# Index keys and head weights of the second layer: weight columns stationary, tokens moving

## The reference, cut to what matters

```python
h = _rmsnorm(x, ln_mix_g[l])
proj = h @ w_in[l]
(aq, ak, av, iq, ik, iw, hq, ...) = _split_cols(proj)
...
wi = wi * (IDX_HEADS ** -0.5 * IDX_DIM ** -0.5)
...
sc = jax.nn.relu(jnp.einsum('bqhd,bsd->bqhs', qi_b, ki))        # 4 heads x 64
sc = jnp.einsum('bqhs,bqh->bqs', sc, wi_b).astype(jnp.float32)
...
_, idx = lax.top_k(sc, n_sel)
```

## Time and profile before

| what | value |
|---|---|
| median of the timed runs | 1281.21 us |
| the three runs | 1283.12, 1279.31, 1281.21 us |
| profiled execution, from its first to its last instruction (span) | 1275.6 us |
| the profiled execution's own time as a run | not listed beside the span |
| PE busy | 1195.1 us (94%) |
| DVE / ACT / POOL busy | 642.8 / 478.1 / 207.0 us |
| product `ikw`, from its first matmul to that of `akv` | 784.97 to 792.80 us |
| product `akv`, from its first matmul to that of `aq` | 792.80 to 806.16 us |

### The profile page before, as it was taken

The page is one execution under the profiler, slowest core; times in us unless marked ns, Lnnn a source line. Parts: engine busy times, 40 slices in busy tenths (PEclk is TensorE's granted clock), DMA queues, the critical chain, the costliest instruction groups (busy, mean ns, idle before and its releaser), DMA issues.

```text
span 1275.6 us, 16095 instructions
## 1 busy us (share of the span) xinstructions
PE 1195.1 (94%) x6536; PEld 854.7 (67%) x6536; DVE 642.8 (50%) x949; ACT 478.1 (37%) x741; POOL 207.0 (16%) x190
## 2 busy tenths in 40 slices
PE   7998999999988998999999988999999889999998
PEld 7986754344435986654444435889887767988996
DVE  3897631212125678712222116596489885445544
ACT  3596421111103466311010113475566534444442
POOL 6000000000002000000000000087788550000000
PEclk9999989999999999789999998999999999999999
DMA  9900879999998531789999993533334342264450
GB/s 332 331 1 1 332 294 431 426 428 428 426 420 280 195 140 59 292 371 427 427 428 427 428 406 130 198 132 133 132 136 176 140 144 79 119 238 159 181 215 33
DMA packets 68162, 321.23 MB, mean 252 GB/s; under 512 B 4071, under 2 KB 12660, under 8 KB 55418
## 3 DMA queue, kind: packets, MB, share of 16 engines
q1 hardware_dynamic: 64944, 308.57, 61.1%
q0 software_dynamic: 2592, 11.42, 2.6%
q10 hardware_dynamic: 554, 0.23, 0.1%
HBM read 317.02 MB, written 3.18 MB: 251 GB/s over the span
## 4 chain that ended last, share of the span: by engine, by line
PE 70%; DVE 15%; DMA 5%; ACT 4%; issue 3%; POOL 2%; DVEq 0%; SPq 0%; ACTq 0%
PE bank L1529 32%; PE bank L1712 23%; PE bank L1594 4%; PE bank L1703 3%; DMA arena<-in_moe_w_up_dram 2%; POOL w_lo L666 2%; DMA ring<-in_w_kv_dram 2%; PE bank L1761 2%; DVE w_lo L666 2%; PE bank L1497 1%; ACT w_hi L953 1%; DVE arena L2298 1%; DVE rows L2852 1%; DVE arena L2871 1%; PE bank L1601 1%
## 5 line engine op out<-in xcount | busy, mean ns | idle before, releaser
L666 POOL TENSOR_TENSOR w_lo<-ring,w_hi 128x512 fp32r<-128x512 f32 (+1 forms) x124 | 178.1, 1469 | 659.3 <-ACT w_hi L953 659.3
L953 ACT ACTIVATE w_hi<-ring 128x2048 fp32r<-128x2048 f32 (+1 forms) x102 | 191.9, 1883 | 213.0 <-PE bank L1529 211.5
L666 DVE TENSOR_TENSOR w_lo<-ring,w_hi 128x2048 fp32r<-128x2048 f32 x71 | 160.8, 2266 | 150.4 <-ACT w_hi L953 149.9
L1529 PE MATMUL bank<-x_hi,w_hi 128*128 128x256 f32 x672 | 112.0, 289 | 3.9 <-DVE x_lo L2253 2.2
L1529 PE MATMUL bank<-x_hi,w_lo 128*128 128x256 f32 x672 | 108.9, 284 | 1.2 <-POOL w_lo L666 1.0
L1529 PE MATMUL bank<-x_lo,w_hi 128*128 128x256 f32 x672 | 108.3, 284 | 0.0
L1529 PE MATMUL bank<-w_hi,x_hi 128*128 128x512 f32 (+1 forms) x336 | 96.7, 403 | 10.8 <-DVE x_lo L2633 3.6
L1712 PE MATMUL bank<-arena 128*64 128x512 f32 x352 | 98.6, 594 | 1.9 <-ACT arena L953 1.8
L1529 PE MATMUL bank<-w_lo,x_hi 128*128 128x512 f32 (+1 forms) x336 | 94.4, 396 | 4.3 <-POOL w_lo L666 4.3
L1529 PEld LDWEIGHTS bank<-x_hi,w_hi 128*128 128x128 f32 x672 | 93.2, 193 | 6.5 <-issue 6.0
L953 ACT ACTIVATE arena<-bank 128x512 f32<-128x512 f32 (+3 forms) x85 | 40.0, 486 | 148.5 <-PE bank L1745 103.9
(11 more groups left out here) (333 smaller groups left out, 1776.9 us busy)
## 6 DMA issues: line engine op xcount, KB each, us to landing
ring<-in_w_in_dram SPq DMA_DIRECT2D x15, 2048.0 KB, 7.8
ring<-in_moe_w_gate_dram SPq DMA_DIRECT2D x12, 2048.0 KB, 20.0
arena<-in_moe_w_down_dram SPq DMA_DIRECT2D x12, 2048.0 KB, 21.8
arena<-in_moe_w_gate_dram SPq DMA_DIRECT2D x12, 2048.0 KB, 17.1
ring<-in_moe_w_down_dram SPq DMA_DIRECT2D x12, 2048.0 KB, 18.4
ring<-in_moe_w_up_dram SPq DMA_DIRECT2D x12, 2048.0 KB, 17.6
arena<-in_moe_w_up_dram SPq DMA_DIRECT2D x12, 2048.0 KB, 21.4
wslots<-in_moe_w_up_dram SPq DMA_DIRECT2D x8, 2048.0 KB, 22.5
```

The costliest lines, as they stand in the source:

```text
L666: last = ops.tensor_tensor(part(w_lo, label, hb)[:, x].bitcast(F32R), ring_half(label, hb)[:, x], part(w_hi, label, hb)[:, x], ALU.subtract)
L953: return s.activation(dst, src, ACT.Copy)
L1529: last = mm(bank(use_)[:, at:at + cols], still, moving, start=start and opens and (hb, n, k) == (0, 0, 0), stop=stop and closes and (hb, n ...
```

## The change

The product `ikw` is made with the 68 weight columns stationary and all 256 tokens moving, in one unit instead of two, into partitions 0 to 67 of one bank. ACT copies the 64 key rows out of it twice, to partitions 0 to 63 and 64 to 127 of `ikT`, and the 4 weight rows into a new tile `iwT`; these three copies stand in ACT's program behind both `w_hi` of `akv` and ahead of `w_hi` half 0 of `aq`. PE transposes the two 4-row pieces of `iwT` back (4 columns each) where it transposed `ikd`, and DVE scales them out of PSUM into `iws` behind the remainders of `hf`. The five DVE operations and the tiles `ikw` and `ikd` go, and so does ACT's copy of `ikT`. In `split_product` the signal `hi_read` moves, for a product with one unit only, from the last matmul of the second term to the first of the third. Nine semaphores are folded into others that are counted on; no instruction is added by that.

```diff
-        add("ikw", wide(win, C_IK, IKW), IKW, ("ikw", NT - 1))
+        add("ikw", wide(win, C_IK, IKW), IKW, ("ikw", 0))
...
             highs("akv")
+            ready(act, ("ikw", 0))
+            for twice in range(2):
+                copy(ikT[twice * HD:(twice + 1) * HD, :], bank(("ikw", 0))[0:HD, 0:T])
+            free(copy(iwT[HD:IKW, :], bank(("ikw", 0))[HD:IKW, 0:T]), ("ikw", 0))
             high("aq", 0)
...
             free(copy(iqT, bank("iqT")[:].rearrange("p (c t) -> p c t", c=2)), "iqT")
-            ready(act, "ikT")
-            free(copy(ikT, bank("ikT")[:, 0:T]), "ikT")
...
-                            last = mm(bank(use_)[:, at:at + cols], still, moving,
+                            last = mm(bank(use_)[0:still.shape[1], at:at + cols], still, moving,
                                       start=start and opens and (hb, n, k) == (0, 0, 0),
                                       stop=stop and closes and (hb, n, k) == (1, 2, rows_ - 1))
-                        if n == 1 and closing:
+                            if n == 2 and k == 0 and opening and closing:
+                                last.then_inc(hi_read[hb], 1)
+                        if n == 1 and closing and not opening:
                             last.then_inc(hi_read[hb], 1)
...
-                    pe.wait_ge(sem("ikd"), 1)
-                    pieces("ikT", [lambda t: ikd[:, t, :]])
+                    claim(pe, "iwT")
+                    freed(pe, ("ikw", 0))
+                    for t_ in range(NT):
+                        last = tr(bank("iwT")[:, t_ * IDX_HEADS:(t_ + 1) * IDX_HEADS], iwT[HD:IKW, t_ * P:(t_ + 1) * P],
+                                  ident[HD:IKW, HD:IKW])
+                    full(last, "iwT")
...
-            linear_tok("ikw", "ikw", IKW, arrives="rm0")
+            split_product("ikw", [(("ikw", 0), T, slice(0, T), slice(0, IKW))], False, arrives="rm0")
             linear_tok("akv", "akv")
             linear_tok("aq", "aq", steps=during_aq)
-            for label in ("iqT", "ikT"):
-                freed(pe, label)
+            freed(pe, "iqT")
...
             low(dve, v, "akv", 0)
-            for t in range(NT):
-                ready(dve, ("ikw", t))
-                free(v.tensor_copy(ikw[:, t, :], bank(("ikw", t))[:, 0:IKW]), ("ikw", t))
-            freed(dve, ("ikw", NT - 1))
-            v.tensor_scalar(iws, ikw[:, :, HD:HD + IDX_HEADS], IDX_HEADS ** -0.5 * HD ** -0.5, None, ALU.mult)
-            v.tensor_copy(ikd[:, :, 0:HD], ikw[:, :, 0:HD])
-            v.tensor_copy(ikd[:, :, HD:], ikw[:, :, 0:HD]).then_inc(sem("ikd"), 1)
-            dve.wait_ge(sem("ikd"), 1)
             low(dve, v, "akv", 1)
...
             low(dve, v, "hf", 1)
+            ready(dve, "iwT")
+            free(v.tensor_scalar(iws, bank("iwT")[:, 0:NT * IDX_HEADS].rearrange("p (t h) -> p t h", t=NT),
+                                 IDX_HEADS ** -0.5 * HD ** -0.5, None, ALU.mult), "iwT")
+            freed(dve, "iwT")
```

The folded semaphores, one of them as an example (`over_known`, the halves of `k` and `q`, the gain rows, `chosen` and `gates` go the same way):

```diff
-            pool.dma_start(bias1.rearrange("p h k -> p (h k)"), biases.ap()[:, 0, :]).then_inc(sem("bias1"), 16)
+            pool.dma_start(bias1.rearrange("p h k -> p (h k)"), biases.ap()[:, 0, :]).then_inc(sem("bias"), 16)
...
-                    dve.wait_ge(sem("bias2"), 16)
+                    dve.wait_ge(sem("bias"), 32)
```

More of the change, by code:

```diff
@@ L230, in program @@
         ikT = take(T)
-        ikd = take(NT, 2 * HD)
+        iwT = take(T)
         A_AQ = take.at[0]
@@ L241, in program @@
         iscore = take(NT, T)
-        ikw = take(NT, IKW)
         qh = take(HH, T)
@@ L458, in program @@
         use_transposes("rm0")
-        for name, b in (("ikw", 0), ("akv", 2), ("aq", 0)):
+        use(("ikw", 0), 0)
+        for name, b in (("akv", 2), ("aq", 0)):
             for t in range(NT):
@@ L462, in program @@
         use("iqT", 4)
-        use("ikT", 5)
+        use("iwT", 5)
         for qt in range(NT):
@@ L689, in spilled @@
         def spilled(eng, l):
-            eng.wait_ge(sem(f"over_known{l}"), 1)
+            eng.wait_ge(sem("over_known"), l + 1)
             return eng.value_load(over_any[l][0:1, 0:1], min_val=0, max_val=1)
@@ L743, in load @@
                     to = block(label).rearrange("p k (m n) -> p k m n", m=2)
-                    for m, signal in enumerate((sem(f"{name}{g}_half"), slot_landed[b["slot"]])):
+                    for m, signal in enumerate((sem(f"{name}_half"), slot_landed[b["slot"]])):
                         sp.dma_start(to[:, :, m, :], src[:, :, m, :]).then_inc(signal, 16)
@@ L894, in load_rows @@
                     pool.dma_start(rows[n % 2][:, k, :], src[l:l + 1, :].broadcast_to([P, D]))\
-                        .then_inc(sem(f"rows{n}"), 16)
+                        .then_inc(sem(f"rows{n % 2}"), 16)
             load_rows(0)
@@ L919, in _ @@
             pool.wait_ge(sem("ln3_tok"), NT)
-            pool.dma_start(bias2.rearrange("p h k -> p (h k)"), biases.ap()[:, 1, :]).then_inc(sem("bias2"), 16)
+            pool.dma_start(bias2.rearrange("p h k -> p (h k)"), biases.ap()[:, 1, :]).then_inc(sem("bias"), 16)
             r4 = reset.rearrange("p h (c t) -> p (h c) t", t=CHUNK)
@@ L992, in high @@
                     if label[0] in ("k", "q"):
-                        act.wait_ge(sem(f"{label[0]}{label[1]}_half"), 16)
+                        act.wait_ge(sem(f"{label[0]}_half"), 16 * (label[1] + 1))
                 if splits[label] != (0, 0):
@@ L1677, in experts @@
                 warm(("rank", l), 2)
-                pe.wait_ge(sem(f"chosen{l}"), 1)
+                pe.wait_ge(sem("chosen"), l + 1)
                 r = bank(("rank", l))
@@ L1775, in experts @@
                     gathered(0, r)
-                pe.wait_ge(sem(f"gates{l}"), 1)
+                pe.wait_ge(sem("gates"), l + 1)
                 selected(0)
@@ L2360, in tile_rows @@
                 r = rows[0]
-                dve.wait_ge(sem(f"rows{n[2:]}"), 32)
+                dve.wait_ge(sem(f"rows{int(n[2:]) % 2}"), 32 * (int(n[2:]) // 2 + 1))
                 dve.wait_ge(sem(f"{n}_var"), t + 1)
@@ L2444, in experts @@
                                                  in_group[:, t, 0:1], keep[:, g_, :], ALU.is_equal, ALU.mult)
-                ins.then_inc(sem(f"chosen{l}"), 1)
-                dve.wait_ge(sem(f"chosen{l}"), 1)
+                ins.then_inc(sem("chosen"), 1)
+                dve.wait_ge(sem("chosen"), l + 1)
                 link(v.tensor_tensor(gates16.rearrange("p t e -> p (t e)"), place.rearrange("p g e -> p (g e)"), aff,
@@ L2452, in experts @@
                 v.tensor_tensor(gates16, gates16, bcast(gsum.unsqueeze(2), NT, EXPERTS), ALU.mult)\
-                    .then_inc(sem(f"gates{l}"), 1)
+                    .then_inc(sem("gates"), 1)
                 def by_hidden(x):
@@ L2489, in experts @@
                 link(v.tensor_reduce(over[:, EXPERTS:EXPERTS + 1], over[:, 0:EXPERTS], AX, ALU.max))
-                v.tensor_copy(over_any[l][0:1, :], over[0:1, EXPERTS:EXPERTS + 1]).then_inc(sem(f"over_known{l}"), 1)
+                v.tensor_copy(over_any[l][0:1, :], over[0:1, EXPERTS:EXPERTS + 1]).then_inc(sem("over_known"), 1)
                 more = spilled(dve, l)
@@ L2645, in _ @@
             low(dve, v, ("v", 0), 1)
-            dve.wait_ge(sem("bias1"), 16)
+            dve.wait_ge(sem("bias"), 16)
             logits(0)
```

## The result

The changed kernel takes 1273.65 us (median of 4 runs, 1272.18 to 1275.16), the kernel before 1280.26 us beside it (4 runs). The ratio is 0.9946, 95% interval 0.993 to 0.9963: 6.6 us less. Timed once more in twelve runs on another occasion it gave 0.9958 (0.9944 to 0.9971), 5.4 us. In medians that is 6.0 us (1280.12 to 1274.08). The forecast was 6.0 us less, 1275.2 us. The span of the profiled execution went from 1275.6 to 1270.5 us, 5.1 less. The execution with the 1270.5 us span took 1272.18 us as a run, so its time is 1.7 us above the span. In 31 timed executions of the kernel before, the time is 1.7 to 2.2 us above the span too. So the profiled one of the kernel before stands for some 1277.3 to 1277.8 us: of the 5.6 us between its span and the median, 3.4 to 3.9 were differences between executions, and it was one of the faster ones.

The account below looks back on a forecast made before the run. PE, busy 94% of the span, bounds the kernel, with `ikw` and `akv` partly at low clock. `aq` 6.5 to 5.9 us sooner, plus 0.2 for `iws`, gives -6.0: 1281.21 to 1275.2 us, range 1272 to 1281.

Parts of the forecast that it names:

- the two waits: PE at the head of `akv`, waiting for ACT's `w_hi` half 0 and then DVE's remainder: about 0.35 and 0.5 us idle.
- The lower bound of 0.086: Pace of the `ikw` matmuls if the stationary load set it, 0.086 us each; 0.8 us shorter than at 0.120, but hidden.
- The estimate from the fast weight load: `ikw`: if 68 stationary columns lost the fast load, the product could take some 4.8 us, 1.9 more than summed.
- the low stretch that goes: `ikw` and `akv`: 1.2 GHz clock from 787.6 to 797.8, about 5 us lost; forecast to vanish or last some 3.4 us.
- The plain reading of the Trainium skill: Rival: clock follows PE busy time, so stays low from 787.6 to 797.8 as before; gain 2.6 less 0.2, 1278.8; chance 0.13.
- The 17 us at 531 to 548: Earlier low-clock place, cited as the clock staying low under 16-wide matmuls with PE busy without a pause.
- Both courses of the forecast: Clock at `ikw` and `akv`: stays up, `aq` 6.5 us sooner; or falls for 3.4 us, `aq` 5.9 us sooner.
- DVE's 0.2 us: New `iws` ahead of the score sums, in DVE's unbroken work up to `qk_norm`: no slack, full 0.2 us counted as cost.
- ACT's three copies: Added ACT work from 790.1 to 791.4, about 1.3 us; no cost, since `w_hi` half 0 of `aq` waits for PE anyway.
- The transposes: PE's transposes of `iwT` replace two of six; between no cost and a wide one's lie 0.2 us; zero gain taken.
- Given back later: Rival: everything behind meets clock falls elsewhere or a wait; two more falls cost 3.4 us, net -2.6, 1278.6; chance 0.08.
- The slower case: Rival: PE's two new waits in `akv` bring a long low clock; 17 us of it gives +2.2, 1283.4; chance 0.07.

## Why the prediction was right

**The product.** 24 x 0.120 = 2.88 us was expected, and PE has 0.120 and the two waits where they were forecast, 0.29 and 0.22 us of idle PE for 0.35 and 0.5; the second was sized too large. `aq` was forecast at 799.65 (the terms add to 799.57) and starts at 799.78. The lower bound of 0.086 wasn't reached: with few moving columns the pace is 0.062, but 256 moving columns set 0.120 themselves. The estimate from the fast weight load of the Trainium skill (TensorE: Matmul & The Clock Gate, "Weight-path perf modes") was 4.8 us; the product took 2.9, so 68 stationary columns lost nothing. That estimate has a gap: twice 192 ns a load is 0.384 us and 9.2 for the product, and its 0.2 us a matmul fits only if the load is also scaled to 68 of 128 columns. No load of that length came.

**The clock.** About 5 us of the gain is the low stretch that goes, as worked out (21.19 - 16.25 = 4.9); the rest of the 6.3 us is the pace of the product less the two waits (16.25 - 14.85 = 1.4). That wide moving tiles are the reason was an inference from a few places of one trace; the experiments bear it out. Narrow tiles in the new orientation bring the stretch back with the same falls ahead, which is the strongest of them; wide ones in the old orientation lose it, by one profile; PE is busy all the while in both. The plain reading of the Trainium skill (the same page, "The HAM clock gate") by busy time alone would have had the clock go alike in them; the measurement decides against it.

One row was read too simply. The 17 us at 531 to 548 were put down to 16-wide matmuls with PE busy. These take 5.7 us of it (from 533.55 to 536.99 and from 541.00 to 543.30), 512-wide ones and transposes lie between, and behind them the clock stayed low for another 5.4 us of 256-wide ones:

```profile
...
536.99 3.76 PE L1497 MATMUL bank<-blockmask,ident 128*128 128x512 f32 x4
541.00 0.61 PE L1680 MATMUL bank<-small,earlier 128*128 128x16 f32 x2 [0.25 <-DVE small L2443]
...
543.30 0.88 PE L1703 MATMUL bank<-sel_r,tok_hi_r 128*128 128x256 f32 x2
...
548.67 0.41 PE L1703 MATMUL bank<-sel_r,tok_hi_r 128*128 128x256 f32 x2
...
```

So this place doesn't show by itself that narrow tiles hold the clock down, nor do 256-wide ones always bring it back in 3.4 us. The argument rests on `ikw`.

Both courses of the forecast occur: no fall (14.84 or 14.85 us to `aq`) in four profiles of the changed form without filling ahead or with two, and one short fall (15.32) in one.

**The added work.** DVE's 0.2 us has nearly the right size where it is paid, 0.12 to 0.15, but it wasn't paid in the first profiled pair. There PE lost 0.33 us ahead of this place to POOL's remainder (839.29 to 840.53, where four such matmuls take 0.91), a term that the forecast didn't have. ACT's three copies took 1.13 us (1.3 expected) and lie ahead of a pause of 2.65 us. The transposes were mis-sized: I took no change, but from the first `iqT` transpose to the second half of `aq` PE now needs 0.74 us (805.23 to 805.97) where six wide ones took 0.57 (811.61 to 812.18). The transposes with the two 4-column ones cost 0.17 us more than those with the wide ones. So the net before the later falls is 6.36 - 0.17 - 0.33 = 5.9 us; 6.0 was forecast. That it agrees to 0.1 us is luck in part: the 0.17 and POOL's wait weren't in the sum, DVE's 0.2 was, and the second wait in `akv` was sized too large.

**Given back later.** This was a rival with 3.4 us, and it happened with 0.8 in the profiled pair (a lead of 5.9 became 5.1). It isn't part of the change: where the clock falls in the last 270 us differs between executions of one kernel, by 3.3 us of span in the two of the changed one. From `aq` to the end the distance grew by 1.3 us (469.4 to 470.7), less than the 2 us named as a sign of being wrong. The times of more executions give 5.4 to 6.6, on either side of the forecast.

**The slower case** didn't occur: the two new waits of PE in `akv` brought no fall in any profile of the changed kernel. A low stretch of 10 us came back only with the 64-wide tile, whose kernel is 2.5 us slower than the kernel before in the median (1283.16 to 1280.62).

## What to carry to other kernels

When one operand of a product has few columns, let them stand still and move the long side: a narrow moving tile pays the pace of its 128 stationary columns, and here it held the clock down into the wide matmuls behind it. Read the granted clock for a stretch before pricing its matmuls, and price the wall time at the clock that they will have. Time such a change over ten runs or more; falls of the clock elsewhere move single executions by as much as the change does.

## What the hardware showed unexpectedly

With 68 stationary columns, 64 and 128 moving columns cost the same, 0.062 us a matmul at the full clock; 256 cost 0.120. With 128 stationary columns, 68 moving ones cost 0.1115. The clock fell behind 5.3 us of matmuls without any idle time, 68 columns wide each, and stayed at 2.4 GHz through 48 matmuls of 128 columns 0.062 us apart, which last only 3.0 us. Four executions of three kernels came to the same product with the same falls behind them; 64 and 68 moving columns were followed by 10.2 us of low clock, 256 by none. Two executions of one kernel, 3.3 us apart in span, differed by 6.7 us of low clock, and half of that is 3.4 us.
